# Output projection of the later token tiles between the pairs of the first FFN group, turns by DMA, and another order of queues

## What is computed

```python
def trunk_layer(x, c, pool_buf, conv_buf, ffn_buf, pos0, ...):
    mod = (jax.nn.silu(c) @ w_ada + b_ada)[:, None, :]
    sh1, sc1, gt1, sh2, sc2, gt2 = jnp.split(mod, 6, axis=-1)
    h = rmsnorm(x, g_pre_mix) * (1 + sc1) + sh1
    proj = h @ w_in
    v_pool, x_conv, gate_b, gate_c = jnp.split(proj, [512, 1024, 1536], axis=-1)
    pool_in = jnp.concatenate([pool_buf, v_pool], axis=1)
    y_pool = pool_mixer(pool_in, pos0, pool_w, pool_scale)    # trailing windows 2, 4, 8, 16
    conv_in = jnp.concatenate([conv_buf, gate_c * x_conv], axis=1)
    y_conv = gate_b * causal_dwconv(conv_in, conv_w)          # three taps along the tokens
    mix = jnp.concatenate([y_pool, y_conv], axis=-1) @ w_out
    x = x + gt1 * rmsnorm(mix, g_post_mix)
    h2 = rmsnorm(x, g_pre_ffn) * (1 + sc2) + sh2
    up = h2 @ ffn_w_up
    ffn_in = jnp.concatenate([ffn_buf, up], axis=1)
    a, b = jnp.split(causal_dwconv(ffn_in, ffn_conv_w), 2, axis=-1)
    f = (jax.nn.silu(a) * b) @ ffn_w_down
    x = x + gt2 * rmsnorm(f, g_post_ffn)
    return x, pool_in[:, -15:], conv_in[:, -2:], ffn_in[:, -2:]
```

## Time and profile before

| what | us |
|---|---|
| median of 3 runs (792.25 to 793.2) | 792.54 |
| the profiled execution's own time | 792.03 |
| its span, on the slowest core (7) | 790.5 |
| spans of the 8 cores | 783.1 to 790.5 |
| PE busy | 710.0 (90%) |
| DVE, ACT, POOL busy | 471.6, 328.5, 261.0 |

### The profile page before, as it was taken

One profiled execution on the slowest core, in us unless ns is written; L12 is line 12 of the kernel. 1 busy time (PEld: TensorE's weight loads), 2 busy tenths in 40 slices (PEclk: granted clock), 3 DMA queues, 4 the chain that ended last, 5 costly groups with the idle time before them and its releaser, 6 DMA issues.

```text
span 790.5 us, 12158 instructions; the slowest of 8 cores (783.1 to 790.5 us)
## 1 busy us (share of the span) xinstructions
PE 710.0 (90%) x4051; PEld 339.4 (43%) x4051; DVE 471.6 (60%) x618; ACT 328.5 (42%) x577; POOL 261.0 (33%) x238
## 2 busy tenths in 40 slices
PE   1287887997999879899999999999999999999995
PEld 0143443443444434344444444444444444444442
DVE  1357886352657765867777741116788787779112
ACT  3406854141456565454445421115444444523211
POOL 5003303231354552444434332223233333243230
PEclk9999999999999999999999999999999999999998
DMA  8996607899857668365855763210442443032341
GB/s 181 222 175 151 187 1 114 148 202 178 182 137 244 231 181 208 64 136 97 153 115 103 139 158 133 107 54 27 80 82 54 83 78 54 1 107 86 114 144 43
DMA packets 26863, 97.92 MB, mean 124 GB/s; under 512 B 3075, under 2 KB 7515, under 8 KB 23202
## 3 DMA queue, kind: packets, MB, share of 16 engines
q0 software_dynamic: 9792, 47.85, 34.7%
q1 hardware_dynamic: 17010, 49.31, 19.3%
HBM read 126.15 MB, written 19.19 MB: 184 GB/s over the span
## 4 chain that ended last, share of the span: by engine, by line
PE 70%; DMA 13%; DVE 6%; issue 5%; ACT 3%; POOL 2%; SPq 1%; DVEq 0%; POOLq 0%; ACTq 0%
PE ps L394 68%; DMA ring_62<-w_gate 4%; DMA big_65<-x 4%; DVE ah_71 L429 2%; DMA y<-big_65 2%; DMA big_68<-x 1%; DMA stgf_108<-st_ffn 1%; PE ps L591 1%; DVE big_69 L419 1%; DMA big_69<-w_ss 1%; POOL big_68 L423 1%; PE ps L402 1%; DVE stat_53 L506 0%; ACT ah_71 L415 0%; DVE xn_81 L428 0%
## 5 line engine op out<-in xcount | busy, mean ns | idle before, releaser
L394 PE MATMUL ps<-ah_71,ring_64 128*128 128x512 bf16 (+1 forms) x880 | 167.8, 345 | 4.3 <-DVE ah_71 L534 1.5
L394 PE MATMUL ps<-wdn_120,g_119 128*128 128x512 bf16 (+1 forms) x748 | 162.7, 379 | 0.0
L394 PE MATMUL ps<-ah_71,ring_63 128*128 128x512 bf16 (+1 forms) x816 | 153.4, 341 | 7.0 <-DVE by_72 L423 2.3
L394 PE MATMUL ps<-ah_71,ring_62 128*128 128x512 bf16 (+1 forms) x656 | 124.7, 345 | 6.4 <-DVE big_66 L419 3.2
L394 PEld LDWEIGHTS ps<-ah_71,ring_64 128*128 128x128 bf16 x880 | 74.8, 98 | 86.9 <-issue 9.0
L394 PEld LDWEIGHTS ps<-wdn_120,g_119 128*128 128x128 bf16 (+1 forms) x748 | 73.3, 99 | 86.9 <-issue 0.8
L394 PEld LDWEIGHTS ps<-ah_71,ring_63 128*128 128x128 bf16 x816 | 69.1, 98 | 84.3 <-issue 11.4
L506 DVE RECIPROCAL stat_53<-stat_53 128x1 f32<-128x1 f32 (+1 forms) x68 | 10.3, 159 | 141.4 <-ACT stat_53 L415 141.2
L394 PEld LDWEIGHTS ps<-ah_71,ring_62 128*128 128x128 bf16 x656 | 56.6, 98 | 70.7 <-issue 9.8
L423 POOL TENSOR_TENSOR g_119<-big_65,big_66 128x1024 bf16<-128x1024 f32 x15 | 35.4, 2357 | 69.0 <-DVE big_66 L423 36.3
L423 POOL TENSOR_TENSOR g_119<-big_67,big_68 128x1024 bf16<-128x1024 f32 x15 | 35.4, 2359 | 64.4 <-DVE big_68 L423 31.8
(11 more groups left out here) (296 smaller groups left out, 893.9 us busy)
## 6 DMA issues: line engine op xcount, KB each, us to landing
ring_64<-w_up POOLq DMA_DIRECT2D x8, 1024.0 KB, 8.4
ring_63<-w_up POOLq DMA_DIRECT2D x7, 1024.0 KB, 8.6
ring_62<-w_up POOLq DMA_DIRECT2D x7, 1024.0 KB, 8.6
wdn_120<-w_down POOLq DMA_DIRECT2D x11, 512.0 KB, 10.4
y<-big_67 SPq DMA_DIRECT2D x9, 512.0 KB, 2.6
ring_62<-w_gate POOLq DMA_DIRECT2D x4, 1024.0 KB, 14.1
y<-big_68 SPq DMA_DIRECT2D x8, 512.0 KB, 3.5
y<-big_65 SPq DMA_DIRECT2D x8, 512.0 KB, 2.9
```

Of the source, the lines that this page charges most:

```text
L394: inst = e.matmul(bank_ap, l, r, start=(first and i == 0), stop=(last and i == len(pairs) - 1))
```

## The change

**What it does.**
- `order()` takes, instead of what was recorded first, what is needed first: an operation's key is the record number of the earliest PE operation that depends on it, directly or through others, and then its own. DMAs have a list of their own per engine. At most 1.2 MB are under way (5 MB if the load is the most urgent of all; loads up to 0.4 MB go at any time). Each DMA also gets a dependency on the transfer that landed last in the model before its issue, so that the chip waits for it too.
- `turn_tile` becomes one DMA on SP that transposes a tile from `XN` to `AH`. It is used for tiles 8 to 16 before the mixer and for all 17 of the output projection, there one step after the tile's `norm_tile`. The first eight tiles keep PE's turn (`turn_tile_pe`). `XN` has three buffers for four.
- In the mixer the conv units of columns 0 and 1 (j = 0 and 1) stand ahead of tiles 8 to 11, `pool_mid` is cut in `pool_evac` and `pool_win`, `ada2` chunks 0 to 3 are loaded early (two into `BY`), `gate_rows` is cut in halves that are spread over the conv units. `w_out` has buffers of its own (`WO`).
- Only the first 11 tiles (`NFIRST`) of the output projection stand ahead of the FFN. The other six, with the steps that drain, go one per pair between the pairs of `up_group(0)`. `GB` now lies behind `WDN`, so that the first 11 pairs (`NTAIL`) write where nothing is still read. `w_down` is loaded from pair 11 on, and the FFN's carried rows are loaded and turned at pairs 12 and 15 (`ffn_states`).

```diff
+    LIMIT, SHARE, SMALL = 5.0e6, 1.2e6, 0.4e6
     def order(self):
...
+        for o in reversed(self.all):
+            need[o] = o.idx if o.eng == "pe" else min([far] + [need[u] for u in users[o]])
+            o.key = (need[o], o.idx)
...
-                if not busy[e] and ready[e]:
-                    _, o = heapq.heappop(ready[e])
-                    busy[e] = True
-                    self.ops[e].append(o)
-                    o.start = t
-                    push(t + o.cost, "free", o)
+                src = ready[e] if ready[e] else None
+                if loads[e] and (src is None or loads[e][0][0] < src[0][0]):
+                    o = loads[e][0][1]
+                    first = min(h[0] for h in loads.values() if h)[1]
+                    cap = self.LIMIT if o is first else self.SHARE
+                    if under == 0.0 or o.nbytes <= self.SMALL or under + o.nbytes <= cap:
+                        src = loads[e]
+                if src is None:
+                    continue
+                o = heapq.heappop(src)[1]
...
+                if o.dma:
+                    under += o.nbytes
+                    if last is not None:
+                        o.deps.add(last)
...
             else:
+                under -= o.nbytes
+                last = o
                 done(o)
...
-    NXN = 4
+    NXN = 3
...
+    WDN = alloc("wdn", [128, NPAIR, D], BF16)
+    g_at = cur[0]
     GB = alloc("g", [128, NPAIR, GW], BF16)
-    WDN = alloc("wdn", [128, NPAIR, D], BF16)
+    E1 = alloc("e", [128, D], F32)
+    NTAIL, NFIRST = 11, 11
+    wo_at = g_at + NTAIL * 2 * GW
+    WO = [alloc("wo", [128, KC, 512], BF16, at=wo_at + 8192 * i) for i in range(2)]
...
-    def turn_tile(t, j, eng):
+    def turn_tile_pe(t, j, eng):
...
+    def turn_tile(t, j):
+        r0, rows = tile_rows(t)
+        K.dma("sp", lambda e: [e.dma_start_transpose(out=AH[:, :, r0:r0 + rows], in_=XN[j][0:rows, :])], s_xn[j], 1,
+              reads=[r_xn[j]], writes=[r_ah[kc][t] for kc in range(KC)], nbytes=rows * 3000)
...
+    for j, c in ((0, 0), (0, 1), (1, 0), (1, 1)):
+        conv_unit(j, c)
+    tiles_in(2)
+    conv_unit(0, 2)
+    pool_out(0)
+    pool_unit(2)
+    conv_unit(1, 2)
+    tiles_in(3)
...
+    todo = {(2, 0): [lambda: pool_states(), lambda: gate_rows(0, 0)], (2, 1): [lambda: ada2(4, 4)],
+            (2, 2): [lambda: ada2(5, 5), lambda: gate_rows(0, 1), lambda: gate_load(0)], (2, 3): [lambda: ada2(6, 4)],
+            (2, 4): [lambda: ada2(7, 5)], (3, 0): [lambda: gate_rows(1, 0)], (3, 3): [lambda: gate_rows(1, 1)]}
...
-    for step in range(17 + 5):
-        if step < 17:
+    def o_step(step, lo, hi):
+        if step < hi:
             o_mm(step)
...
-        t = step - 3
-        if 0 <= t < 17:
-            turn_tile(t, o_xn[t], "act" if t % 2 else "dve")
+        t = step - 2
+        if lo <= t < hi:
+            turn_tile(t, o_xn[t])
...
+    for step in range(NFIRST):
...
+        o_step(step, 0, 17)
...
     def up_group(gi):
         for i in range(NPAIR):
+            if gi == 0:
+                while out_steps and (len(out_steps) > 19 - NFIRST - i or i == NTAIL - 1):
+                    o_step(out_steps.pop(0), 0, 17)
...
+                if i == NTAIL + 1:
+                    ffn_states(7, 0, 8)
+                if i == NTAIL + 4:
+                    ffn_states(7, 8, 11)
```

More of the change, by code:

```diff
@@ L127, in order @@
                 users[d].append(o)
+        far = len(self.all)
+        need = {}
+        for o in reversed(self.all):
+            need[o] = o.idx if o.eng == "pe" else min([far] + [need[u] for u in users[o]])
+            o.key = (need[o], o.idx)
         ready = {e: [] for e in self.ENGS}
+        loads = {e: [] for e in self.ENGS}
         busy = {e: False for e in self.ENGS}
@@ L134, in order @@
         t = 0.0
+        under = 0.0
+        last = None
         def push(at, kind, o):
@@ L138, in push, with add @@
             heapq.heappush(events, (at, seq[0], kind, o))
+        def add(o):
+            heapq.heappush((loads if o.dma else ready)[o.eng], (o.key, o))
         def done(o):
@@ L148, in order @@
             if not waiting[o]:
[L149 removed]
+                add(o)
         left = len(self.all)
@@ L693, in pool_mid, with pool_win @@
             act(V[:, 16:528], PSF[:, b, :], AF.Copy, [r_bank[b]], [rV], n)
-            give(b)
+        else:
+            act(VS[:, g, :, PB:PB + DS], PSF[:, b, 0:TS].rearrange("p (s r) -> p s r", r=DS), AF.Copy, [r_bank[b]], [r_vs], TS)
+        give(b)
+    def pool_win(g, c):
+        c0, n = COLT[c]
+        w = WIN[g]
+        d = d_i[0] % 3
+        d_i[0] += 1
+        if c < 4:
+            V, rV = VB[g][c % 2], r_v[g][c % 2]
             S = SB_[g]
@@ L736, in build_program @@
     conv_n = [0]
-    r_ql = R()
+    r_ql = [R() for _ in range(4)]
     conv_op = {}
@@ L783, in conv_mid, with ada2 @@
         give(bb)
-    pend = []
-    def flush(n=0):
-        while len(pend) > n:
-            pool_end(*pend.pop(0))
+    s_w2 = [new_sem("w2_%d" % i) for i in range(4)]
+    def ada2(kc, i):
+        if i < 2:
+            buf, r_buf, sem = BY[:, 6 + i, 0:2048], R(r_wss1), next_misc()
+            for r in r_by[6 + i]:
+                r.alias([r_buf])
+        else:
+            buf, r_buf, sem = BIG[i].bitcast(BF16), r_big[i], s_w2[i - 4]
+        load(buf, wss_d[1, kc], [r_buf], 1 << 20, eng="pool", sem=sem)
+        ada_vec(buf.rearrange("p (a k n) -> p a k n", a=2, k=KC), r_buf, kc, G2T, S2T, r_m2, 8, V_GFFN, V_BADA + 16)
+        if i < 2:
+            for r in r_by[6 + i]:
+                r.alias([r_buf])
@@ L982, in build_program @@
     up_op = []
+    out_steps = list(range(NFIRST, 19))
     def load_wdn(q):
@@ L1024, in up_group @@
                         up_load(gi, q)
-                if gi == 0:
-                    for q in range(max(0, (pb - 1) * 12 // 10), min(11, pb * 12 // 10)):
+                if gi == 0 and i >= NTAIL:
+                    k = (i - NTAIL) // 2
+                    for q in range(2 * k, 11 if k == 4 else 2 * k + 2):
                         load_wdn(q)
```

274 lines of the change are left out of this document (140 added, 134 removed).

## The result

The changed kernel takes 816.8 us (median; 813.4 to 818.2) where the kernel before takes 792.4 on the same chip (791.0 to 793.2): a ratio of 1.030, 95% interval 1.027 to 1.034. It is 3.0% slower. The forecast was 764.5 us, its range 748 to 800: wrong in sign and outside of the range.

What follows compares the result with a forecast made beforehand. DMA was taken as full up to 61.5 us, TensorE as the bound behind 320.7. From 790.5 us, 53.3 went off before the FFN and 20.7, 1.6 and 3 came back; with 1.5 and 0.5 added, 764.5 us, range 748 to 800.

Steps and rivals of the forecast that it cites:

- What bounds the kernel: Whole kernel: only the first 320.7 us can give anything; behind them TensorE bounds and only its own work counts.
- The start, 0: Start, up to 61.5 us: DMA engines are full, so reordering the same bytes gives 0, ends -3 and +10 us.
- rival b: POOL's weight loads up to w_out: bounded transfers starve the DMA engines, first tile at 232 at worst, 778 to 796; chance 0.20.
- The sum: Whole kernel: 790.5 - 53.3 + 20.7 + 1.6 + 3 + 0 = 762.5 us of span, 764.5 us in all.
- The 10.6 us of waits go: Mixer: TensorE's waits on gate weights, a modulated tile, FFN state and a w_ss chunk vanish, 10.6 us less.
- late next: Mixer: DVE's modulation of tiles 8 to 11 waits for four transposes, ahead of conv work; no time added.
- The transposes: Turns by DMA: landing after 5.4 us, ends 2.6 and 22.9; free with three XN buffers up to 8.4 us.
- rival c: Mixer and output projection: slow transposes and three XN buffers set the pace, up to 829.5 us; chance 0.15.
- 7.6 us idle: Before the FFN: TensorE waits for tile 7's 19 us chain, of which tiles 8 to 10 cover 11.4.
- 3.8 us: Output projection: time per tile without its turn, 41.8 us for 11 tiles; no engine forbids it.
- "3 us" in the first group: First FFN group: six tiles between pairs should hide; 3 us allowed for mixing, bounds 0 and 8.5 us.
- 53.3 us less before the FFN: Up to the FFN: start at 250.2 against 303.5, where an FFN that never stalled would have started.

Runs made afterwards that it cites:

- after: The changed kernel as first measured, with the whole change in place, against the kernel before: 816.8 us, ratio 1.030.
- the repairs: Changed kernel with landed waits only in the model's first 40 us and the output projection's first x tiles in free buffers: 793.5 us, 1.000 of before.
- (7): Output projection's 17 turns put back on TensorE in the kernel with the repairs: 802.8 us with 11 tiles ahead of the FFN, 806.0 with 13.

## Why the prediction was wrong, step by step

**What bounds the kernel**: right. The loss lies before the first `w_down` matmul, and the rest took as long as before.

**The start, 0**: right (62.0). That the bound was needed for it was not seen.

**The landed waits** (rival b): the mechanism was in the text, in the wrong place. It was costed as gaps between POOL's loads up to `w_out`, with its sign in the first 60 us. There the DMA share stayed at 0.99, and the waits gain; behind the start they cost 19 us. The sum had them at 0. The mixer's late landings belong to this term: without the waits the longest falls from 22.0 to 11.6 us, and TensorE's longest sum of waits there from 29.4 to 14.6. Why a landed wait makes a transpose land later was not traced.

**"The 10.6 us of waits go"**: failed in after. The longest wait on `w_gate` fell from 7.6 to 3.9 us, where the prediction wanted none over 2, and late transposes brought two new ones, 13.0 us through ACT and an XN buffer and 6.5 through DVE. The text named DVE's modulation as "late next" and priced it at nothing; ACT's wait it did not name here. With the repairs the first output tile of the slowest core comes at 205.3: 12.6 us earlier than before (217.9), of 16.2 forecast.

**The transposes** (rival c): 5.4 us was assumed, the median is 4.5, but the longest is 22.0. The rival's mechanism, an XN buffer held until the landing, came once in the mixer and cost TensorE 13.0 us on core 4. The pace that it priced (27 us in the mixer, 38 in the output projection) did not come: the transposes of the output projection landed after 3 to 7 us. The turn by DMA was right for the mixer; in the output projection it is 9 us better than TensorE's (7). The estimate from the Trainium skill (DMA: Bandwidth & Descriptors, "Latency and other measured facts"), 3 us, is the least landing measured.

**"7.6 us idle" before the FFN**: failed. Two things were left out: that x tiles lie in the second gate's buffers (10.7 us at once in after; 4.0 of time, since the next wait takes over), and that tiles do not follow the matmuls at 3.8 us. TensorE waits 16.5 us in the output projection of after, and with the repairs 17 us at the FFN's start. My sum of engine times, each of which fits in 3.8 us, says that no engine is full; it does not say that a chain of nine steps over ACT, DVE, POOL and a transfer, with three XN buffers and in-order queues, keeps that pace. That the chain's pace is the cause of the waits is the reading that is left, and no run shows it by itself.

**"3 us" in the first group, bounds 0 and 8.5**: failed, and with the repairs it is what is left of the error. 20.7 us were measured in after, 24 to 28 with the repairs; the prediction itself had called a loss above 8.5 us there a sign of being wrong. The part known is 4.7 us of table loads. I took the mixing before (25.6 us for 17.2) as an upper bound, though only five groups of matmuls stood there. Which resource holds the chain is open: cover, SP's turns, x buffers and mixing were each changed, and the 25 us stayed, in one place or the other. The three XN buffers were not changed.

**The sum**: 53.3 us less before the FFN was the term that carried the forecast. It counts from 303.5, where an FFN without gaps would have started; by the first FFN matmul it is 44.9 (295.1 less 250.2). With both repairs 34 to 38 of these come (260.8 for 295.1 on the slowest cores, 250.1 for 288.4 on the fastest), and the first group gives them back: 198 to 201 us for 161.5 before (456.6 - 295.1), of which the six tiles are 20.7.

In short, four terms failed. The landed waits stood at 0 and cost 19 us. Of the 10.6 us of waits only a part went, and 19.5 us of new ones came on core 4. The 7.6 us before the FFN measured 16.5, and the 3 us in the group 20.7. For the last two the runs show the size and not the resource behind it.

## What to carry over

When work moves from a place where one engine was full into a place where five engines hand over to each other, cost the chain's pace (its longest loop through buffers and queues) beside each engine's load; the busy shares can all look free. And ask of each buffer which engine stands still until its transfer has landed. In these runs a wait on a landing paid only where all bytes competed for the same moment. Look also for what the moved work alternates with on ACT: each change of function set is a load.

## What the runs showed of the hardware

A transpose by DMA of 128 x 1024 bf16 landed after 3.0 us at best. The latest of the mixer landed after 12.3 to 22.0 us on the cores of after, after 7.1 to 11.6 in the run without landed waits; three stand in a row in both, so the row alone does not make the 22. The 26 transposes make 26496 more packets under 512 B (29571 less 3075), about 1000 each: without the nine of the mixer they are 8992 fewer, without the 17 of the output projection 17440. The DMA engines of core 4 looked busy and moved little while two of the late ones were under way: from 81.7 to 103.7 us a share of 1.28 and 112 GB/s, where the start has 0.99 and 198.

SP's issue of one grew from 1.2 to 5.9 us there, and what stood behind it in SP's queue waited.

TensorE's mean clock was some 0.94 on two neighbouring cores in three of the four executions of the run with 11 tiles ahead and two gated buffers: on cores 0 and 1 twice, on 4 and 5 once. In the profiled one the lower clock lasted for a whole stage. Windows of its core 0 and then of core 6:

```profile
200.00:340.00 140.00, 125.56 (x486) 52.36 (x495) 77.58 (x113) 71.51 (x132) 51.43 (x29) 0.80 0.78 183
...
200.00:340.00 140.00, 112.65 (x474) 48.31 (x482) 86.22 (x117) 78.95 (x142) 55.61 (x29) 0.93 0.77 187
```

For about as many matmuls core 0 was busy 12.9 us longer. What sets this off was not tried.
